# TensorE takes half of the first modulation of a hybrid encoder layer, straight from the loaded rows

## The reference

```python
mod = (silu(c) @ w_mod[l] + b_mod[l])[:, None, :]          # c: (1, 1024), w_mod: (1024, 6 * 1024)
sh_m, sc_m, gt_m, sh_f, sc_f, gt_f = jnp.split(mod, 6, axis=-1)
h = rms_norm(x, g_pre_mix[l]) * (1.0 + sc_m) + sh_m
y = hybrid_mixer(h, w_in[l], ...)                          # proj = h @ w_in, (512 x 1024) @ (1024 x 7168)
x = x + gt_m * rms_norm(y, g_post_mix[l])
h = rms_norm(x, g_pre_mlp[l]) * (1.0 + sc_f) + sh_f
y = square(relu(h @ w_mlp_up[l])) @ w_mlp_down[l]          # 1024 -> 4096 -> 1024
x = x + gt_f * rms_norm(y, g_post_mlp[l])
```

## Time and profile before

| | us |
|---|---|
| median of 3 runs | 849.56 (848.59 to 849.98) |
| profiled execution, span from the first to the last instruction | 846.6 |
| TensorE busy with matmuls | 819.2 |
| VectorE busy | 459.7 |
| ScalarE busy | 379.5 |
| GpSimd busy | 19.8 |

### The profile page before, as it was taken

How to read it: one execution, slowest core, us unless ns; L and a number is a source line. 1 busy time by engine, 2 the same in 40 slices (tenths; PEclk the granted TensorE clock), 3 DMA queues, 4 the chain that set the end, 5 groups by cost and what they waited for, 6 DMA issues and landing times.

```text
span 846.6 us, 10887 instructions
## 1 busy us (share of the span) xinstructions
PE 819.2 (97%) x3714; PEld 682.4 (81%) x3714; DVE 459.7 (54%) x598; ACT 379.5 (45%) x530; POOL 19.8 (2%) x21
## 2 busy tenths in 40 slices
PE   3699999999999999999999999999999999999997
PEld 3578888888888888888888898888888888888885
DVE  5966776666676556555774664333333433333335
ACT  6337777666665444444343653222222322222233
POOL 2311000000000000000000000000000000000000
PEclk9699999999999999999999999999999999999999
DMA  9934333325068666666337034333332223233202
GB/s 306 316 107 107 106 105 105 105 81 180 25 190 237 180 188 197 198 194 178 124 125 224 14 87 125 99 99 99 99 99 90 89 95 100 99 99 99 99 0 99
DMA packets 136438, 109.42 MB, mean 129 GB/s; under 512 B 3925, under 2 KB 120801, under 8 KB 136417
## 3 DMA queue, kind: packets, MB, share of 16 engines
q1 hardware_dynamic: 136192, 109.10, 42.9%
q0 software_dynamic: 160, 0.04, 0.0%
q10 hardware_dynamic: 64, 0.02, 0.0%
HBM read 107.04 MB, written 2.10 MB: 129 GB/s over the span
## 4 chain that ended last, share of the span: by engine, by line
PE 93%; DVE 4%; ACT 1%; DMA 1%; issue 1%; SPq 0%; DVEq 0%; ACTq 0%
PE ps L330 31%; PE ps L331 31%; PE ps L332 31%; DVE mod L837 3%; DMA xs<-in_x_dram 1%; ACT junk L506 1%; PE ps L1265 0%; PE ps L1165 0%; DVE ht_lo L883 0%; DVE k_pos L818 0%; PE ps L1238 0%; PE ps L1237 0%; ACT xnt L531 0%; ACT ht_hi L533 0%; DVE xnt L859 0%
## 5 line engine op out<-in xcount | busy, mean ns | idle before, releaser
L788 DVE TENSOR_TENSOR w_lo<-raw,w_hi 128x1024 fp32r<-128x1024 f32 x131 | 160.2, 1224 | 63.4 <-ACT w_hi L493 56.7
L330 PE MATMUL ps<-ht_hi,w_hi 128*128 128x512 f32 x448 | 177.0, 395 | 3.0 <-DVE ht_lo L883 3.0
L331 PE MATMUL ps<-ht_lo,w_hi 128*128 128x512 f32 x448 | 176.5, 394 | 0.0
L332 PE MATMUL ps<-ht_hi,w_lo 128*128 128x512 f32 x448 | 176.0, 393 | 0.0
L493 ACT ACTIVATE w_hi<-raw 128x1024 fp32r<-128x1024 f32 x132 | 138.3, 1050 | 37.6 <-PE ps L332 31.2
L330 PE MATMUL ps<-h_hi,w_hi 128*128 128x512 f32 (+1 forms) x288 | 105.5, 366 | 0.0
L331 PE MATMUL ps<-h_lo,w_hi 128*128 128x512 f32 (+1 forms) x288 | 105.4, 366 | 0.0
L332 PE MATMUL ps<-h_hi,w_lo 128*128 128x512 f32 (+1 forms) x288 | 105.4, 366 | 0.0
L330 PEld LDWEIGHTS ps<-ht_hi,w_hi 128*128 128x128 f32 x448 | 85.3, 190 | 20.7 <-issue 3.0
L332 PEld LDWEIGHTS ps<-ht_hi,w_lo 128*128 128x128 f32 x448 | 85.3, 190 | 18.0
L330 PE MATMUL ps<-w_hi,hd_hi 128*128 128x512 f32 x256 | 99.7, 390 | 0.0
(11 more groups left out here) (181 smaller groups left out, 1012.3 us busy)
## 6 DMA issues: line engine op xcount, KB each, us to landing
raw<-in_w_in_dram SPq DMA_DIRECT2D x52, 512.0 KB, 4.8
modraw<-in_w_mod_dram SPq DMA_DIRECT2D x32, 512.0 KB, 4.2
raw<-in_w_mlp_up_dram SPq DMA_DIRECT2D x32, 512.0 KB, 4.1
raw<-in_w_mlp_down_dram SPq DMA_DIRECT2D x32, 512.0 KB, 3.3
mod_raw<-in_w_mod_dram SPq DMA_DIRECT2D x16, 512.0 KB, 6.6
xs<-in_x_dram SPq DMA_DIRECT2D x8, 512.0 KB, 6.3
raw<-in_w_a_out_dram SPq DMA_DIRECT2D x8, 512.0 KB, 5.3
raw<-in_w_b_out_dram SPq DMA_DIRECT2D x8, 512.0 KB, 5.7
```

The source lines that it names most:

```text
L330: nc.tensor.matmul(dst, l_hi, r_hi, start=first, stop=False)
L331: nc.tensor.matmul(dst, l_hi, r_lo, start=False, stop=False)
L332: return nc.tensor.matmul(dst, l_lo, r_hi, start=False, stop=last)
L788: V.tensor_tensor(w_lo[:, slot, :], raw[:, slot, :], f(w_hi[:, slot, :]), ALU.subtract).then_inc(w_lo_ready, 1)
```

## The change

TensorE takes over the second half of each pair. VectorE keeps the input blocks 0 to 3 (16 steps in all). For the blocks 4 to 7 `mod0_columns` has 4 more plain float32 matmuls for each of its 4 columns, 16 for each call: the stationary operand is a 128 x 128 piece of the loaded rows themselves, the moving one a column of `c_act`, and they accumulate behind the matmul with ones. The row buffers become five, the two new ones in space that is free in the opening. Even ones are freed by VectorE's steps, odd ones by the column sums, and `load_gates(0)` waits for the last column sums. VectorE's program has the steps of a pair in fewer places, and the last softplus steps stand behind `ht_lo`.

```diff
--- before.py
+++ after.py
@@ -125,8 +125,9 @@
         sig_a = at("sig_a", [P, SEQ], O_GS + ROW)
         picked = at("picked", [P, HALF // P, P], O_GS)[:, :, :]
 
-        M0_BUFS = 3
-        mod0_raw = at("mod0_raw", [P, M0_BUFS, NB // 2, 2, 2 * P], O_YB)
+        M0_BUFS = 5
+        mod0_raw = [at(f"mod0_raw{b}", [P, NB // 2, 2, 2 * P], off)
+                    for b, off in enumerate((O_YB, O_YB + 8 * KIB, O_YB + 16 * KIB, O_YA + 16 * KIB, O_YA + 24 * KIB))]
         mod0 = at("mod0", [P, 2, D], O_YB + 24 * KIB)
         vrows = at("vrows", [P, P], O_MB)
         crows = at("crows", [NB, P], O_MB + KIB)
@@ -183,6 +184,8 @@
         mod0_in0 = sem("mod0_in0")
         mod0_in1 = sem("mod0_in1")
         mod0_in2 = sem("mod0_in2")
+        mod0_in3 = sem("mod0_in3")
+        mod0_in4 = sem("mod0_in4")
         raw0a_in = sem("raw0a_in")
         raw0b_in = sem("raw0b_in")
         raw0c_in = sem("raw0c_in")
@@ -306,7 +309,7 @@
         z_out = sem("z_out")
         raw_in = [raw_in0, raw_in1, raw_in2, raw_in3]
         xr_in = [xr_in0, xr_in1, xr_in2, xr_in3]
-        mod0_in = [mod0_in0, mod0_in1, mod0_in2]
+        mod0_in = [mod0_in0, mod0_in1, mod0_in2, mod0_in3, mod0_in4]
         modraw_in = [modraw_in0, modraw_in1]
 
         SP_STEPS = 16
@@ -358,11 +361,15 @@
             def load_mod0(i):
 
 
-                wait(sp_eng, mod0_acc, NB // 2 * (i - M0_BUFS + 1))
+                before = i - M0_BUFS
+                if before >= 0 and before % 2 == 0:
+                    sp_eng.wait_ge(mod0_acc, NB // 2 * (before // 2 + 1))
+                elif before >= 0:
+                    sp_eng.wait_ge(mod0_sum, before // 2 + 1)
                 ks = slice(i % 2 * NB // 2, (i % 2 + 1) * NB // 2)
                 for a in range(2):
                     col = a * D + i // 2 * 2 * P
-                    sp_eng.dma_start(mod0_raw[:, i % M0_BUFS, :, a, :],
+                    sp_eng.dma_start(mod0_raw[i % M0_BUFS][:, :, a, :],
                                      w_mod_v[:, ks, col:col + 2 * P]).then_inc(mod0_in[i % M0_BUFS], 16)
 
             def load_first_units(ks, semaphore):
@@ -389,7 +396,7 @@
             load_unit(RING + 1, 1, w_in_v[:, :, COL_C + P:COL_C + 2 * P])
             load_unit(RING + 2, 2, w_in_v[:, :, COL_V + P:COL_V + 2 * P])
             load_unit(RING + 3, 3, w_in_v[:, :, COL_B + P:COL_B + 2 * P])
-            sp_eng.wait_ge(mod0_acc, NB // 2 * NB)
+            sp_eng.wait_ge(mod0_sum, NB // 2)
             load_gates(0)
 
             with sp_eng.Fori(2, NB) as n:
@@ -820,23 +827,23 @@
                     ins = V.tensor_scalar(k_neg[:, :], k_pos[:, :], -1.0, None, ALU.mult)
                 ins.then_inc(sp_step, 1)
 
-            def mod0_steps(i, steps=range(NB // 2), softplus_from=None):
-
-                if i >= NB:
+            def mod0_steps(p, steps=range(NB // 2), softplus_from=None):
+
+                if p >= NB // 2:
                     return
+                i = 2 * p
                 if steps.start == 0:
                     dve.wait_ge(mod0_in[i % M0_BUFS], 32 * (i // M0_BUFS + 1))
-                acc = mod0[:, :, i // 2 * 2 * P:(i // 2 + 1) * 2 * P]
-                for m in steps:
-                    k = i % 2 * NB // 2 + m
-                    part = mod0_raw[:, i % M0_BUFS, m, :, :]
+                acc = mod0[:, :, p * 2 * P:(p + 1) * 2 * P]
+                for k in steps:
+                    part = mod0_raw[i % M0_BUFS][:, k, :, :]
                     if k == 0:
                         V.tensor_scalar(acc, part, c_act[:, 0:1], None, ALU.mult).then_inc(mod0_acc, 1)
                     else:
-                        dve.wait_ge(mod0_acc, i // 2 * NB + k)
+                        dve.wait_ge(mod0_acc, p * (NB // 2) + k)
                         V.scalar_tensor_tensor(acc, part, c_act[:, k:k + 1], acc, ALU.mult, ALU.add).then_inc(mod0_acc, 1)
                     if softplus_from is not None and softplus_from < SP_STEPS:
-                        softplus_step(softplus_from + m)
+                        softplus_step(softplus_from + k)
 
             mod0_steps(0)
             dve.wait_ge(cols_sum, 1)
@@ -850,7 +857,6 @@
                 V.reciprocal(stat[:, 8 + t:9 + t], stat[:, 4 + t:5 + t]).then_inc(x_rstd, 1)
                 dve.wait_ge(x_rstd, t + 1)
                 V.tensor_scalar(xs[:, t, :], xs[:, t, :], stat[:, 8 + t:9 + t], None, ALU.mult).then_inc(x_norm, 1)
-            mod0_steps(1)
             dve.wait_ge(x_tr, NB)
 
             def evacuate(banks):
@@ -863,7 +869,7 @@
             for p in range(NB // 2):
 
                 if p > 0:
-                    mod0_steps(2 * p + 2, range(0, 2), softplus_from=8 * p)
+                    mod0_steps(p + 1, range(0, 2), softplus_from=8 * p)
                 dve.wait_ge(mod0_sum, p + 1)
                 k = 2 * p
                 V.tensor_tensor(mcol[:, k:k + 2], ps[:, B_T1, k:k + 2], cols[:, C_BS + k:C_BS + k + 2], ALU.add).then_inc(col0_ready, 1)
@@ -873,14 +879,15 @@
                 if p == 0:
                     evacuate((4, 5))
                 else:
-                    mod0_steps(2 * p + 2, range(2, 4), softplus_from=8 * p)
+                    mod0_steps(p + 1, range(2, 4), softplus_from=8 * p)
                 for k in (2 * p, 2 * p + 1):
                     if k == 1:
-                        mod0_steps(2, softplus_from=0)
-                    if k % 2 == 1:
-                        mod0_steps(2 * p + 3, softplus_from=8 * p + 4)
+                        mod0_steps(1, softplus_from=0)
                     dve.wait_ge(h_hi, k + 1)
                     V.tensor_tensor(ht_lo[:, k, :], xnt[:, k, :], f(ht_hi[:, k, :]), ALU.subtract).then_inc(h_lo, 1)
+                    if k % 2 == 1 and 8 * p + 4 < SP_STEPS:
+                        for m in range(NB // 2):
+                            softplus_step(8 * p + 4 + m)
             dve.wait_ge(w_lo_ready, split_count(RING))
             split_lo(RING + 1, 1)
             dve.wait_ge(sp_step, SP_STEPS + 1)
@@ -1159,11 +1166,16 @@
 
             def mod0_columns(p):
 
-                pe.wait_ge(mod0_acc, NB * (p + 1))
+                i = 2 * p + 1
+                pe.wait_ge(mod0_in[i % M0_BUFS], 32 * (i // M0_BUFS + 1))
+                pe.wait_ge(mod0_acc, NB // 2 * (p + 1))
                 for j in (2 * p, 2 * p + 1):
                     for a in range(2):
-                        last = nc.tensor.matmul(ps[:, B_T1, a * NB + j:a * NB + j + 1], mod0[:, a, j * P:(j + 1) * P],
-                                                ones[:, 0:1], start=True, stop=True)
+                        dst = ps[:, B_T1, a * NB + j:a * NB + j + 1]
+                        nc.tensor.matmul(dst, mod0[:, a, j * P:(j + 1) * P], ones[:, 0:1], start=True, stop=False)
+                        for m in range(NB // 2):
+                            last = nc.tensor.matmul(dst, mod0_raw[i % M0_BUFS][:, m, a, (j - 2 * p) * P:(j - 2 * p + 1) * P],
+                                                    c_act[:, NB // 2 + m:NB // 2 + m + 1], start=False, stop=m == NB // 2 - 1)
                 last.then_inc(mod0_sum, 1)
 
             pe.wait_ge(xnt_ready, 1)
```

## The result

The changed kernel takes 863.29 us (median of 4 runs, 862.17 to 866.92), the one before 849.22 beside it. The ratio is 1.0172, with a 95% interval of 1.0150 to 1.0194: 1.7% slower, 14 us. I had forecast 855.6 us, 6 us slower. The direction was right, the size was not: the change costs more than twice what the sum said. The time lies in the range, near its upper end, where rival (A), the clock, had put it.

What follows compares the result with a forecast made beforehand. TensorE's matmuls bound the kernel, VectorE its opening; four calls add 14.2 us of records, and block 5 moves from 54.82 to 61.0 us, +6.2. Forecast 849.6 + 6.0 = 855.6 us, range 852.0 to 866.

Steps and rivals of the forecast that it cites:

- rival (A): Clock falls low behind calls 2 to 4, two or three stretches: 862 to 866 us; chance 0.28.
- step (4): Calls 2 to 4 and products of blocks 1 to 4 at high clock: block 5 at 61.0 us, 6.2 later.
- What bounds the opening: Opening, before 55 us: VectorE is the slowest engine; its modulation multiply-adds hold 31.7% of the chain.
- The ceiling of 10.6 us: TensorE's idle time in the opening, 5.8 + 3.0 + 1.8 us, as the most to win; the 3.0 stays.
- The price of a record: Column-sum calls: two records per float32 matmul, 0.111 us each at high clock; 3.55 us added per call, 14.2 for four.
- (C): Row-buffer loads pipeline better, at 0.083 us, and the clock stays high: block 5 at 51.8, 846.5 us; chance 0.04.
- (E): Four loads for each added matmul, or worse clocks throughout: 870 us; chance 0.03.
- Steps (1) to (3): Call 1 from 18.15 to 22.75 us, first product 25.75, two VectorE collisions with GpSimd, call 2 at about 33.5.
- (B): One VectorE collision with GpSimd less: second call starts at 31, +3.6, 853.2 us; chance 0.14.
- The rest of the sum: Behind block 5 all work moves as one, adding 0; the forecast is 849.6 + 6.0 = 855.6 us.
- the floor (D): No collision and high clock throughout: block 5 at 56.3, +1.5, 851.1 us; chance 0.05.
- SP's queue, buffers, gates: Row transfers, two extra buffers and gate loads behind the last column sums: hidden, no cost.

Runs made afterwards that it cites:

- experiment 2: The change without its 16 added matmuls per call, so the sums over input blocks 4 to 7 are left out: 842.40 us against 849.06, ratio 0.9924.
- experiment 6: The change with each pair's added matmuls first, ahead of the wait for VectorE's remainder, no fillers: 852.46 us with 64 moving columns, 863.55 with one.
- experiment 7: The kernel before with five buffers and the added matmuls for pair 1 alone: 845.41 us with one moving column, 845.70 with 64.
- experiment 1: The kernel before with five row buffers, all freed by VectorE's steps, arithmetic unchanged: 849.25 us against 849.06, ratio 1.0001.
- e6_warm_narrow: The change, one moving column, with unread filler products in TensorE's gaps ahead of block 0 (12) and call 2 (8): 862.47 us, ratio 1.0174.
- e11_rows_first_1: The change with each pair's added matmuls ahead of the wait for VectorE's remainder, one moving column: 863.55 us, ratio 1.0153.
- e10_rows_first: The change with each pair's added matmuls ahead of the wait for VectorE's remainder, 64 moving columns, no fillers: 852.46 us, ratio 1.0046.
- e9_warm_16: The change with 64 moving columns and unread filler products, 12 ahead of block 0 and 16 ahead of call 2: 854.34 us, ratio 1.0066.
- e2_wide64: The change with 64 equal moving columns instead of one in each matmul of the call: 859.44 us, ratio 1.0104.
- e5_warm_wide: The change with 64 moving columns and unread filler products, 12 ahead of block 0 and 8 ahead of call 2: 860.01 us, ratio 1.0111.
- e1_spread: The change with the added matmuls of pairs 1 to 3 moved in fours between the products of the block before: 859.91 us, ratio 1.0136.

## Why the prediction was wrong in its fourth step

- **What bounds the opening**: right. Halving VectorE's steps by itself gave 6.7 us. The ceiling of 10.6 us was incomplete: it counts TensorE's idle time and leaves out the 5.6 us that TensorE lost to the low clock before, of which experiments 2, 6 and 7 won a part back. My step (4) mentions it as favouring the change, the ceiling does not.
- **The price of a record**: right. Call 1 took 23.06 - 18.43 = 4.6 us, against 4.5; call 4, from 62.6 to 67.1, 4.5; 0.11 us for a record. Two records for a float32 matmul, not four. (C) and (E) fall, since their spacings did not appear.
- **Steps (1) to (3)**: right. The first product stood at 26.02 (25.75 forecast), both collisions came (2.83 and 2.77 us), and call 2 began at 33.47 (33.5 forecast). The Trainium skill (SBUF — State Buffer, "SBUF: two separate sides") says that a VectorE instruction with two SBUF inputs and a GpSimd instruction that reads SBUF take a shared pair of ports as an exclusive lock, for the whole instruction. The trace agrees: VectorE's multiply-add from 26.31 ends at 29.14, behind GpSimd's end at 28.60; GpSimd's next takes 2.84 us instead of 2.42; VectorE's from 29.18 ends at 31.95, again behind GpSimd's end at 31.39. (B), one collision less, falls.
- **Step (4), calls 2 to 4 and the products behind them at the high clock**: this is the step that failed. The sum put the cost of a low clock behind call 2 at nothing, and had block 5 at 61.0 us; it began at 66.99, and one more low stretch lay behind it. The low clock took 8.5 us: three stretches of about 6.8, 6.8 and 3.4 us, half of each lost. Rival (A) had two or three stretches of 6.8 us, 7 to 10 us lost, and so the right mechanism and size; it had a chance of 0.28 against 0.46 for the sum. From the sum's 61.0, two stretches give 61.0 + 6.8 = 67.8, 0.8 more than measured, since a call and its changes of kind cost 0.25 us less than I had summed. In favour of the sum I had taken the transposes' cadence as a sign that loads keep the clock high; but they move 128 columns each, and the granted clock in their rows is 1.00 at both cadences, so the cadence was the only sign. The Trainium skill (TensorE: Matmul & The Clock Gate, Part 4) says that transposes don't count as busy in the same way. The transposes' cadence here, 7 and then 12 in a microsecond, speaks against it for them (whether they use the mode that the page speaks of, the trace does not show); for the calls it pointed to what came.
- **The rest of the sum**: right, shown by the run with fillers and no low clock, 854.34 us against the 855.6 forecast, and by the floor (D), 851.1, beside the 852.46 of the rows-first kernel, whose block 5 began at 58.72 us against the floor's 56.3: call 1 began 0.8 us later than summed, and one low stretch took 1.7. About 1.2 us of the forecast is a wrong base: I set the span of 846.6 beside a median of other runs, 3.0 us above it, while every other run here lies 1.8 to 2.1 us above its own span. The forecast also entered the sum's 6.2 us as 6.0.
- **SP's queue, buffers, gates**: right, nothing (experiment 1, and no wait behind 67 us).

The 14 us (13.8 between the spans) add up: 14.2 us of records, less 5.0 us of idle time (10.6 before, 3.0 + 1.9 + 0.7 = 5.6 after), plus 4.9 us of low clock (it cost 5.6 before; after, 2.0 in block 0 and the 8.5 from above, 10.5).

What lowers the clock is shown by kernels that differ in the moving columns. The low stretches from 20 us on, from the traces:

| run | moving columns | TensorE idle ahead of block 0, of call 2, us | low clock, us |
|---|---|---|---|
| after | 1 | 3.0, 1.9 | 23.1-29.9, 36.8-43.6, 50.4-57.2, 67.5-70.9 |
| `e6_warm_narrow` | 1 | 0, 0 | 22.2-29.1, 39.3-42.7, 49.6-56.4, 66.6-70.0 |
| `e11_rows_first_1` | 1 | 3.0, 0 | 20.9-34.5, 37.9-44.8, 55.0-58.4, 65.3-72.1 |
| `e10_rows_first` | 64 | 3.0, 0 | 27.6-31.0 |
| `e9_warm_16` | 64 | 0, 0 | none |
| `e2_wide64` | 64 | 3.0, 2.2 | 27.4-30.8, 34.2-44.5 |
| `e5_warm_wide` | 64 | 0, 1.9 | 34.9-45.1 |

With one column the clock fell in or behind every call; with 64 it fell only behind idle time. The pair of experiment 6, where nothing but the number of columns differs, shows the first, and the pair of experiment 7 agrees. Idle time alone does not explain it, since `e6_warm_narrow` has none. What idle time does with 64 columns is less certain. With about 2 us of it ahead of call 2 the clock was low in that call in both profiled runs, and with the gap filled it was high; but one of four runs of each kernel took 854.3 us at a mean clock near 1, and 2.1 us of idle time ahead of call 2 in experiment 2, where that call has 8 records, lowered nothing. Whether 64 columns would also raise a low clock stays open; in those two traces it rose only in the products behind the call.

## What to carry to other kernels

Before work is moved to the engine that bounds the kernel, set its whole added time against all that this engine can win, piece by piece. Here 14.2 us stood against 7.6 us of idle time (10.6 less the 3.0 that the change keeps) and 5.6 us of low clock, 13.2 in all: a loss even at best. Taking only the quarter that fits a gap turned a loss of 14 us into a gain of 4. On TensorE, ask of every added stretch how many columns move, not only whether it is busy: a long run of weight loads with one moving column costs its own time and then the clock of the products behind it. If it must stand there, let more columns move, and fill the idle time ahead of it; both kernels that did so here kept the high clock in calls 2 to 4.

## What the runs showed of the hardware

- One plain float32 matmul with a 128 x 128 stationary operand and 1 moving column is two records, 0.22 us together at 2.4 GHz and twice that at 1.2; 64 moving columns cost the same within 2% (3.68 against 3.63 us for 32 records).
- With TensorE 100% busy in the profile, the granted clock fell to 1.2 GHz during or behind 4.5 us of such matmuls with one moving column (`e6_warm_narrow`, four calls of four), and stayed at 2.4 GHz with 64 (`e9_warm_16`, none of four).
- Groups of three products with groups of eight one-column records between them left a low clock low for 15 us and a high one high, in the one trace of `e1_spread`: what held the clock there was not enough to raise it.
- A call of 8 one-column records, 1 us, did not lower a high clock: the kernel before kept it through calls 3 and 4.
- The Trainium skill (TensorE: Matmul & The Clock Gate, "HAM oscillation — how this bites in real kernels") advises against idle gaps between bursts of matmuls. Filling the gap ahead of call 2 agrees with it (`e9_warm_16` against `e5_warm_wide`), but it is not enough: in the one-column kernel of experiment 6 TensorE had no idle gap from block 0 on, and the clock fell three times more.
